# Two input projections with one wide product for the high and low halves of the tokens, and a new order around them

## The reference, cut to what matters

```python
xn = rmsnorm(h, g_pre_mix[l])
proj = xn @ w_in[l]
(s_u, m_q, m_k, m_v, m_o, m_i, m_f, f_q, f_k, f_v, f_f, p_u) = jnp.split(proj, split_idx, axis=-1)
y_ssm = s5_mixer(s_u, ...)                       # a complex linear recurrence, "S5"
y_ml = mlstm_mixer(m_q, m_k, m_v, m_o, ...)      # matrix LSTM; m_o is its output gate
y_fx = fox_mixer(f_q, f_k, f_v, ...)             # attention with forget gates
y_pool = pool_mixer(p_u, pool_w[l], pool_scale[l])
mix = jnp.concatenate([y_ssm, y_ml, y_fx, y_pool], axis=-1) @ w_out[l]
h = h + rmsnorm(mix, g_post_mix[l])
hn = rmsnorm(h, g_pre_ffn[l])
ff = jnp.square(jax.nn.relu(hn @ mlp_w1[l])) @ mlp_w2[l]
```

## Time and profile before

| | |
|---|---|
| median of 3 runs | 3285.32 us (3284.48 to 3285.76) |
| the profiled execution | 3286.47 us, its span 3284.4 us |
| TensorE busy (matmuls) | 3258.7 us, 99% of the span |
| VectorE busy | 1972.3 us, 60% |
| ScalarE busy | 1502.1 us, 46% |
| GpSimd busy | 267.7 us, 8% |
| projections 2 to 9 of block 1 | 58.77 to 288.16 us in the trace |

### The profile page before, as it was taken

How to read it: one execution, slowest core, us unless ns; L and a number is a source line. 1 busy time by engine, 2 the same in 40 slices (tenths; PEclk the granted TensorE clock), 3 DMA queues, 4 the chain that set the end, 5 groups by cost and what they waited for, 6 DMA issues and landing times.

```text
span 3284.4 us, 45113 instructions
## 1 busy us (share of the span) xinstructions
PE 3258.7 (99%) x17342; PEld 2811.9 (86%) x17342; DVE 1972.3 (60%) x2229; ACT 1502.1 (46%) x1755; POOL 267.7 (8%) x211
## 2 busy tenths in 40 slices
PE   8999999999999999999999999999999999999999
PEld 8999888888888888888888888888888888888887
DVE  7898665555555656565555555565656555555555
ACT  5345454434454544544443444454444444444444
POOL 6422000000000034000000000001500000000000
PEclk9999999999999999999999999999999999999999
DMA  7544565655555555455656566655545565556664
GB/s 210 164 132 156 190 205 185 191 187 191 192 193 193 171 182 168 141 189 180 192 183 192 188 192 193 193 178 172 188 145 180 192 192 187 185 190 192 193 192 152
DMA packets 249319, 598.54 MB, mean 182 GB/s; under 512 B 22296, under 2 KB 64248, under 8 KB 248184
## 3 DMA queue, kind: packets, MB, share of 16 engines
q1 hardware_dynamic: 248056, 591.17, 56.6%
q0 software_dynamic: 768, 5.24, 0.4%
q10 hardware_dynamic: 384, 0.58, 0.0%
HBM read 594.86 MB, written 2.10 MB: 182 GB/s over the span
## 4 chain that ended last, share of the span: by engine, by line
PE 96%; DVE 3%; ACT 1%; DVEq 0%; DMA 0%; issue 0%; SPq 0%; ACTq 0%
PE ps L1079 31%; PE ps L653 21%; PE ps L1325 18%; PE ps L659 11%; PE ps L1040 3%; PE ps L727 2%; PE ps L735 2%; PE ps L728 2%; PE ps L1382 1%; PE ps L596 1%; PE ps L1377 1%; DVE wlo L2180 1%; PE ps L1219 0%; PE ps L1217 0%; PE ps L837 0%; DMA x<-in_x 0%
## 5 line engine op out<-in xcount | busy, mean ns | idle before, releaser
L2180 DVE TENSOR_TENSOR wlo<-raw,whi 128x2048 fp32r<-128x2048 f32 (+1 forms) x425 | 971.1, 2285 | 667.6 <-ACT whi L1494 667.1
L1494 ACT CAST whi<-raw 128x2048 fp32r<-128x2048 f32 x425 | 805.2, 1895 | 495.0 <-PE ps L659 426.4
L653 PE MATMUL ps<-xT,whi 128*128 128x512 f32 x3072 | 733.6, 391 | 1.4 <-DVE xT L2198 1.1
L1079 PE MATMUL ps<-whi,stage 128*128 128x512 f32 x3040 | 725.9, 389 | 0.0
L1079 PEld LDWEIGHTS ps<-whi,stage 128*128 128x128 f32 x3040 | 570.4, 188 | 118.1
L653 PEld LDWEIGHTS ps<-xT,whi 128*128 128x128 f32 x3072 | 564.6, 188 | 111.6 <-issue 1.3
L1325 PE MATMUL ps<-whi,xT 128*128 128x512 f32 (+1 forms) x1792 | 444.2, 389 | 1.1 <-DVE wlo L2807 0.9
L659 PEld LDWEIGHTS ps<-xT,wlo 128*128 128x128 f32 x3072 | 393.9, 191 | 14.9
L659 PE MATMUL ps<-xT,wlo 128*128 128x256 f32 x3072 | 398.5, 283 | 0.0
L1887 ACT CAST stage<-big 128x256 fp32r (+1 forms) x384 | 136.9, 404 | 546.6 <-PE ps L1079 535.6
L1079 PE MATMUL ps<-wlo,stage 128*128 128x512 f32 x1520 | 381.1, 389 | 0.0
(11 more groups left out here) (460 smaller groups left out, 2337.6 us busy)
## 6 DMA issues: line engine op xcount, KB each, us to landing
raw<-in_mlp_w SPq DMA_DIRECT2D x128, 1024.0 KB, 5.1
raw<-in_w_up SPq DMA_DIRECT2D x128, 1024.0 KB, 5.3
raw<-in_w_down SPq DMA_DIRECT2D x128, 1024.0 KB, 5.5
raw<-in_w_in SPq DMA_DIRECT2D x100, 1024.0 KB, 5.1
raw<-in_w_o SPq DMA_DIRECT2D x32, 1024.0 KB, 5.6
raw<-in_w_out SPq DMA_DIRECT2D x16, 1024.0 KB, 5.0
raw<-in_w_in SPq DMA_DIRECT2D x16, 832.0 KB, 4.5
raw<-in_w_uq SPq DMA_DIRECT2D x8, 768.0 KB, 4.5
```

Of the source, the lines that this page charges most:

```text
L653: mm(psum(bank + j), whi[:, u % 2, c:c + P], xT[:, k, :], start=k == 0, stop=False)
L1079: return mm(psum(bank + 2 * r + n), x_of(kk, part, r), w[:, u % 2, c:c + 512], start=begin and kk == part == 0 and w is whi, stop=stop)
L1494: act.copy(whi[:, u % 2, 0:width], raw[:, u, 0:width]).then_inc(sig["hi"], 1)
L2180: tt(wlo[:, u % 2, 0:width], raw[:, u, 0:width], whi[:, u % 2, 0:width].bitcast(F32), SUB).then_inc(sig["lo"], 1)
```

## The change

In projections 2 and 9 (`SPARE`), one product of 512 columns takes the place of the two of 272: its moving operand is the 256 high and the 256 low values of the real tokens, side by side. The bank then holds two halves of 256 columns, and the low weight's product (256 columns) goes to the first. Meta tokens are left out in these two projections. ScalarE copies each bank of 512 columns into two tiles of `pT`, one of them spare at that time (tiles of T_MO for projection 2, of T_FK for 9), and VectorE adds four tiles to four in one operation of 128x1024 (`summed`): for projection 2 within projection 3, between `split` 2 and `turn`; for 9 ahead of `ml_args(0)`. The fox scores and the Sigmoid of the output gate wait for it (`sums`, which takes the place of an unused semaphore).

Beside this, the order changes at four places. c_s goes from after panel 2 to between the two tiles of panel 3, in every projection (`BETWEEN_TILES`). In projection 2, panel 0, tile 1 comes ahead of tile 0. In projection 2 on VectorE, `split` of panel 1 comes ahead of `turn_back`. And at the end of the mixer, `added(0, 2)` and `added(1, 2)` come behind the first two `norm_lo` and the first panel of the up projection.

```diff
+BETWEEN_TILES = 5
+SPARE = {2: T_MO, LAST: T_FK}
...
                             hi = whi[:, u % 2, c:c + P]
+                            if q in SPARE:
+                                mm(psum(j).rearrange("p (b n) -> p b n", b=2), hi, xT1[:, k, :, META:L], start=k == 0, stop=False)
+                                continue
...
-                            last = mm(psum(j, L), wlo[:, u % 2, c:c + P], xT1[:, k, 0, :], start=False, stop=k == KD - 1)
+                            n0, n = (META, SEQ) if q in SPARE else (0, L)
+                            last = mm(psum(j, n), wlo[:, u % 2, c:c + P], xT1[:, k, 0, n0:L], start=False, stop=k == KD - 1)
...
-                    for j in range(2):
+                    for j in (1, 0) if q == 2 and u == 0 else (0, 1):
...
                             low(j)
+                        if u == 3 and j == 0 and BETWEEN_TILES in after:
+                            after[BETWEEN_TILES]()
...
+                    pe.wait_ge(sig["sums"], 1)
...
-                after[3].append(lambda: c_s(q - 2))
+                after[BETWEEN_TILES].append(lambda: c_s(q - 2))
...
-                    act.copy(pT[:, PROJECTED[q][1] + 2 * pair + j, :], psum(j, L)).then_inc(sig["evA"], 1)
+                    t = PROJECTED[q][1] + 2 * pair + j
+                    if q in SPARE:
+                        t0, t1 = sorted((t, SPARE[q] + 2 * pair + j))
+                        act.copy(pT[:, t0:t1 + 1:t1 - t0, tok], psum(j).rearrange("p (b n) -> p b n", b=2)).then_inc(sig["evA"], 1)
+                    else:
+                        act.copy(pT[:, t, :], psum(j, L)).then_inc(sig["evA"], 1)
...
             act.wait_ge(sig["evA"], STAGES["w_in1"]["evA"])
+            act.wait_ge(sig["sums"], 2)
...
+            def summed(q):
+                t, spare = PROJECTED[q][1], SPARE[q]
+                dve.wait_ge(sig["evA"], tiles_before(q) + 4)
+                tt(pT[:, t:t + 4, tok], pT[:, t:t + 4, tok], pT[:, spare:spare + 4, tok], ADD).then_inc(sig["sums"], 1)
...
+                if q == 2:
+                    split(Q + q, 1, D)
                 turn_back(s)
-                split(Q + q, 1, D)
+                if q > 2:
+                    split(Q + q, 1, D)
                 if q == 3:
                     gate_sums()
                 scan(s)
                 split(Q + q, 2, D)
+                if q == 3:
+                    summed(2)
                 turn(s)
...
             panel(1)
             panel(2)
+            summed(LAST)
             dve.wait_ge(sig["em"], 1)
             ml_args(0)
...
             closed()
-            added(0, 2)
-            added(1, 2)
             then = norm("pre_ffn", cols[:, V_PRE_FFN:V_PRE_FFN + KD], R_FFN, 2, rope_angles)
             then[0]((0, 1))
             first_panel("up")
+            added(0, 2)
+            added(1, 2)
             then[0]((2, 3))
```

More of the change, by code:

```diff
@@ L386, in build @@
                  "ar", "bt", "bu", "cols", "cpy", "ct", "cv1", "cv2", "dS", "em", "evA",
-                 "evD", "evT", "fe", "fin", "fl", "fmix", "fn", "fp", "fsc", "ft", "fv", "fx", "g2",
+                 "evD", "evT", "fe", "fin", "sums", "fmix", "fn", "fp", "fsc", "ft", "fv", "fx", "g2",
                  "g3", "g4", "g5", "gel", "gn", "gsh", "gst", "hi", "hn", "ld_cst", "ld_dt", "dtr", "ld_gain", "ld_gb",
@@ L923, in hooks @@
             def hooks(q):
-                after = {u: [] for u in range(1, 5)}
+                after = {u: [] for u in (1, 2, 3, BETWEEN_TILES, 4)}
                 if q == 4:
@@ L2478, in fox_tops @@
                     dve.wait_ge(sig["fx"], h)
-                tt(fox_p, psum(6, 416), const("mask_fox"), ADD).then_inc(sig["fl"], 1)
+                tt(fox_p, psum(6, 416), const("mask_fox"), ADD)
                 dve.drain()
```

## The result

The changed kernel takes 3291.97 us (median of 13 runs, 3291.0 to 3295.2), the kernel before in the same session 3284.77 (13 runs, 3284.43 to 3285.76): 7.2 us slower, ratio 1.0023, 95% interval 1.0016 to 1.003. The forecast was 3288.4 in a range of 3280.5 to 3292.5, with "within 0.2%" as the likeliest. The time is at the upper end of the range. The median is just past 0.2% (6.6 us), which the prediction had given a chance of 0.11; the interval has 0.2% inside it, so whether the kernel is slower by more than that is not decided. Of the 7.2 us the sum had 3.1.

The account below looks back on a forecast made before the run. TensorE, holding 96% of the chain, was taken as the bound, with VectorE nearly level. Projections 2 to 8 +2.2, projection 9 and tail +1.9, up projection -1.0: +3.1 us, 3288.4 us, range 3280.5 to 3292.5.

Parts of the forecast that it names:

- The likeliest case: Waits come back at later panels, with 1 to 6 us lost; chance 0.55.
- The up projection: First tiles: moving two added operations behind the first low panel gains 1.0 us of TensorE's 1.11 us wait.
- The products: Projections 2 and 9: wide and smaller low products save 3.3 us of TensorE time, 1.65 a projection.
- waits to 81.35 for lo(2,3): Projection 2, panel 3: TensorE waits from 78.8 for VectorE's low half, 0.55 later than before; projection 0.2 us late.
- waits 2.2: Projection 3, panel 3: TensorE, there at 107.5, waits 2.2 us for VectorE's low half, ready at 109.65.
- so it waits 2.3: Projection 9, panel 3: TensorE arrives after 19.8 us, waits 2.3 for VectorE's low half; projection ends 0.35 us ahead.
- Projection 3: VectorE comes 0.6 us later and adds the 1.15 us sum; c_s again comes behind: 1.6 us newly lost.
- The tail: After projection 9, up to w_out's panel 3: 0.95, 0.4 and 0.9 us lost through ScalarE and VectorE.
- the 0.95 booked at w_out's start: Gelu 1.2 us later and larger evictions 0.4 make w_out's panel 0 0.6 us late: 0.95 new.
- The covers hold: Rival: VectorE and ScalarE are never late, lo(2,3) ready by 78.8; -8.0 us, 3277.3; chance 0.08.
- GpSimd's turns fall better: Rival: most of VectorE's waits for GpSimd meet PSUM-sourced operations; projection 2 gains 2.0 us; 3285.3 in all; chance 0.25.
- ScalarE never became the bound: Rival: ScalarE's chain behind c_s exceeds 4.6 us by 1.0 at each of projections 5 to 8; 3292.0; chance 0.12.

Follow-up runs that it names:

- e9: Changed kernel without wide products and sums; panel 3 of projections 2, 3, 9 issued high 0, c_s, high 1, low 0, low 1: 3282.42 us.
- e10: e9 with the wide products in projection 9 alone, their sum ahead of the pool's outputs: 3282.53 us.
- e3: Kernel before with only the two added operations moved behind the first low panel of the up projection: 3284.11 us.
- e5: Changed kernel with dummy products ahead of the waiting low tiles in projections 2, 3 and 9, each group at most as long as the wait: 3288.88 us.
- e2: Changed kernel without wide products and sums, added operations as before; c_s between panel 3's tiles and projection 2's new order stay: 3288.48 us.
- e1: Kernel before with only the wide products of projections 2 and 9 and their two sums, all reorderings undone: 3287.43 us.
- e6: Changed kernel with only c_s put back between panels 2 and 3 in every projection: 3287.24 us.
- e8: Kernel before with only tile 1 first in panel 0 of projection 2 and VectorE's low half of panel 1 ahead of turn_back: 3285.36 us.

## Why the prediction was right in kind and short by over half

**What held.** The likeliest case was that waits come back at later panels and eat what the products save. The table and e9 against e10 show it. Its own band, 1 to 6 us lost (up to 3291.3), was passed by 0.7 to 1.2 us. Right, too, was the size of projection 3 without the clock, and its step (below). The up projection (-0.9 for -1.0) and the eviction at projection 5 (0.4) were right, e3 confirming the first by itself.

**The products.** Eight wide products took 1.86 us (62.82 to 64.68), eight pairs 2.01 (93.89 to 95.90); with the low ones a projection saves 1.5 us (25.11 against 26.63), where the sum had 1.65. Over 128 the wide products alone give some 2.2 to 2.4 us (in projection 9 of e9 and e10 the high products differ by 1.1). The estimate by the Trainium skill, page "TensorE: Matmul & The Clock Gate", section "Wait — 56ns, not 53.3ns?", was 2.0, nearer than my 2.8. The difference changed nothing, as none of it could be kept.

**The step that failed** is the pricing of each wait in projections 2, 3 and 9 by its length alone: "waits to 81.35 for lo(2,3)", "waits 2.2", "so it waits 2.3". The waits were predicted nearly to size (2.30, 1.66 and 2.60), but TensorE went on at 1.2 GHz behind them. e5 took that away and, as far as its rows show, nothing else: 1.5, 1.3 and 1.6 us, less 1.0 given back at w_out, 3.4 in the stretches and 3.1 in the medians. The sum's +3.1 and these 3.4 make 6.5 of the measured 7.2; that they come so near is partly luck, as the errors below go both ways.

**Projection 3.** I booked the sum on VectorE and c_s' lost cover, +1.6; without the clock's 1.3 it was +1.7. The rows bear out the step: the sum alone made the low half of panel 3 late, by 1.09 us, and c_s follows the wait. What I had wrong is that VectorE would enter the projection late; it was on time. e2, without any sum, has the same stretch (30.00 against 29.95), but by another delay of the same size, the low half of 3.44 us that stood beside GpSimd's operation. In e1 and e6, with c_s early, the low half of panel 3 is 1.7 us late: the sum, and 0.5 us that VectorE was late at low u1 already (4.76 and 4.79 against 4.22). No run has the sum without the wide products.

**Mis-sized.** In projection 2 lo(2,3) came 0.2 us later than before, counted from b_u(0), not 0.55. In projection 9, without the clock, +0.3 instead of -0.35. The tail was +1.4 for +2.25. e1 has 17.16 us there with c_s early, 1.05 more than before, with the sum ahead of ml_args; e2 has 0.8 more with c_s late and no sum; the two don't add up. Of the 0.95 booked at w_out's start, 0.3 came (1.82 us after the pool's products, before 1.54), and it isn't the larger evictions alone: e1 has them too and 1.54.

**The rivals.** "The covers hold" fell: c_s was cover itself, and was moved away, and lo(2,3) was ready at 79.91, not by 78.8. "GpSimd's turns fall better" didn't have its condition met: in projection 2 of the changed kernel four VectorE operations still took 0.3 to 1.0 us longer than their like, among them the low half of 2.59 us and these two of S5's sums, where their like take 0.71:

```profile
64.64 1.56 DVE L2411 TENSOR_TENSOR big<-big 128x544 f32<-128x544 f32 x1
66.12 1.64 DVE L2412 TENSOR_TENSOR big<-big 128x544 f32<-128x544 f32 x1
```

ScalarE never became the bound of projections 5 to 8 (+0.1 in all). The slower end came by a mechanism that no rival had.

**Left open.** Why a wait of 2.20 us leaves the clock full and one of 1.66 doesn't (below). Why e2's executions spread over 5 us. Whether the wide products of projection 2 alone would gain something on top of e9 wasn't tried.

## What to carry to other kernels

Less work on the busiest engine pays only where the next engine's result is there in time; look for the instruction that is cover (here c_s and the high tiles) before moving it, and follow the moved result through the other engines to the last one that waits for it. Issue what needs only early operands ahead of the wait: that order brought some 1.4 to 1.7 us here, and the wide products of projection 9 nothing beside it. An operation that starts late in one place is not yet a cause: count its followers from the start of the stretch they work for, as VectorE's in projection 3, before you give it a price. Where a change lengthens TensorE's waits, price the products behind them at the lower clock as well.

## What the hardware showed that I had not expected

The clock fell behind single waits of 1.66 to 2.60 us, and their length alone doesn't decide it. In the profiled executions the granted clock went from 1.00 to 0.50 after 2.30, 1.66 and 2.60 us (after), 2.05 and 1.76 (e2) and 2.07 at c_s of projection 9 (e1, e6), and stayed full after 2.20 and 2.04 (e1, projections 2 and 3), 1.97 and 2.08 (e6), 1.85 (e8) and 1.72 (before). A fall in the middle of a projection cost 1.3 to 1.6 us (e5 against the changed kernel). Dummy products in the wait kept the clock full in both kernels that had them.
